# Every fourth weight half of the expert stages is split by GpSimd, with a counter of its own

## The reference

```python
def hier_moe(x, w_group, b_group, w_router, b_router, w_gate, w_up, w_down):
    """Two-level routing: top-1 expert group, then top-2 experts inside it; gate = p_group * p_expert."""
    ...
    h = jax.nn.silu(jnp.einsum('td,edf->tef', xf, w_gate)) * jnp.einsum('td,edf->tef', xf, w_up)
    y = jnp.einsum('tef,efd->td', h * gates[:, :, None].astype(h.dtype), w_down)
    return y.reshape(B, S, D)
```

## Time and profile before

| | us |
|---|---|
| median of three runs | 1051.6 (1048.8 to 1054.5) |
| the profiled execution, whole | 1050.4 |
| its span in the trace | 1048.7 |
| TensorE busy | 982.3 (94% of the span) |
| DVE busy | 717.4 (68%) |
| ACT busy | 546.4 (52%) |
| GpSimd busy | 28.3 (3%) |
| first expert stage, in the trace | about 200 to 357 |
| second expert stage | about 507 to 664 |

### The profile page before, as it was taken

How to read it: one execution, slowest core, us unless ns; L and a number is a source line. 1 busy time by engine, 2 the same in 40 slices (tenths; PEclk the granted TensorE clock), 3 DMA queues, 4 the chain that set the end, 5 groups by cost and what they waited for, 6 DMA issues and landing times.

```text
span 1048.7 us, 15179 instructions
## 1 busy us (share of the span) xinstructions
PE 982.3 (94%) x5898; PEld 851.5 (81%) x5898; DVE 717.4 (68%) x865; ACT 546.4 (52%) x603; POOL 28.3 (3%) x65
## 2 busy tenths in 40 slices
PE   8999999999999999997899999997897899999987
PEld 8978988787787798876787787787785899998876
DVE  4788787788689765527888788744554765666575
ACT  4655653467667535551676676433453544444431
POOL 5000010000000000000000000000000000000000
PEclk9999999899999999998999999998999899999999
DMA  9543327299699854412499699554305665555611
GB/s 313 195 162 121 122 93 229 79 324 351 218 364 345 285 195 160 128 42 80 161 326 361 219 345 376 197 166 139 115 7 176 217 199 182 179 173 189 230 51 41
DMA packets 151700, 205.86 MB, mean 196 GB/s; under 512 B 6736, under 2 KB 122960, under 8 KB 151632
## 3 DMA queue, kind: packets, MB, share of 16 engines
q1 hardware_dynamic: 150768, 204.24, 58.2%
q10 hardware_dynamic: 864, 0.70, 0.2%
HBM read 203.86 MB, written 1.05 MB: 195 GB/s over the span
## 4 chain that ended last, share of the span: by engine, by line
PE 77%; DVE 11%; ACT 5%; issue 4%; DMA 2%; POOL 0%; SPq 0%; DVEq 0%; ACTq 0%
PE psum L599 75%; DVE w_lo L1820 5%; ACT w_hi L1387 3%; ACT arena L1387 1%; DVE xt_lo L1837 1%; DMA x_res<-in_x 1%; DMA raw<-in_ffn_w_up 1%; PE psum L704 1%; ACT xt_hi L1387 1%; DVE x_res L2063 1%; PE psum L1036 1%; DVE stats L2068 1%; POOL rstd L462 0%; ACT mt_hi L1387 0%; DVE x_res L2086 0%
## 5 line engine op out<-in xcount | busy, mean ns | idle before, releaser
L1820 DVE TENSOR_TENSOR w_lo<-raw,w_hi 128x2048 fp32r<-128x2048 f32 x184 | 418.2, 2289 | 106.2 <-ACT w_hi L1387 104.2
L1387 ACT ACTIVATE w_hi<-raw 128x2048 fp32r<-128x2048 f32 (+1 forms) x186 | 353.1, 1905 | 116.6 <-PE psum L599 69.8
L599 PE MATMUL psum<-xt_hi,w_hi 128*128 128x256 f32 x704 | 201.7, 287 | 1.8 <-DVEq L2465 1.4
L599 PE MATMUL psum<-xt_hi,w_lo 128*128 128x256 f32 x704 | 199.9, 284 | 0.0
L599 PE MATMUL psum<-xt_lo,w_hi 128*128 128x256 f32 x704 | 199.8, 284 | 0.0
L599 PE MATMUL psum<-w_hi,xt_hi 128*128 128x512 f32 (+1 forms) x432 | 172.2, 399 | 10.3 <-issue 5.7
L599 PE MATMUL psum<-w_hi,xt_lo 128*128 128x512 f32 (+1 forms) x432 | 168.1, 389 | 0.0
L599 PE MATMUL psum<-w_lo,xt_hi 128*128 128x512 f32 (+1 forms) x432 | 167.7, 388 | 0.0
L599 PEld LDWEIGHTS psum<-xt_hi,w_hi 128*128 128x128 f32 x704 | 136.0, 193 | 3.0 <-issue 3.0
L599 PEld LDWEIGHTS psum<-xt_hi,w_lo 128*128 128x128 f32 x704 | 136.0, 193 | 0.0
L599 PEld LDWEIGHTS psum<-xt_lo,w_hi 128*128 128x128 f32 x704 | 135.8, 193 | 0.0
(11 more groups left out here) (246 smaller groups left out, 1220.0 us busy)
## 6 DMA issues: line engine op xcount, KB each, us to landing
raw<-in_w_gate SPq DMA_DIRECT2D x64, 512.0 KB, 4.9
raw<-in_w_up SPq DMA_DIRECT2D x64, 512.0 KB, 6.1
raw<-in_w_down SPq DMA_DIRECT2D x64, 512.0 KB, 5.7
raw<-in_ffn_w_up SPq DMA_DIRECT2D x44, 512.0 KB, 4.6
raw<-in_a_w_in SPq DMA_DIRECT2D x26, 512.0 KB, 6.5
raw<-in_attn_w_in SPq DMA_DIRECT2D x24, 512.0 KB, 5.6
raw<-in_ffn_w_down SPq DMA_DIRECT2D x22, 512.0 KB, 4.3
raw<-in_w_o SPq DMA_DIRECT2D x16, 512.0 KB, 4.6
```

What stands on the lines that cost most here:

```text
L599: return pe.matmul(o, l, r, start=start, stop=stop, skip_group_check=skip)
L1387: return act.activation(o, i, f, **kw)
L1820: return dve.tensor_tensor(w_half(h, w_lo), w_half(h, raw), w_half(h, w_hi).bitcast(F32), ALU.subtract).then_inc(lo_split, 1)
```

## The change

In each expert stage the halves n3, n7 and n11 of every group (`(h - AT[e]) % 4 == 3`) are split by GpSimd, by the same subtraction, and DVE leaves them out. That is 12 halves a layer, 24 in all, of the 96 of the two stages. GpSimd raises `pool_split`; `lo_split` now counts only DVE's halves, and every wait of TensorE and SP is on one or the other counter with a number worked out by `pool_at` and `lo_at`. All of the 24 lie in slot 0 or slot 2 of the ring, one slot per layer. SP's loop over the groups of a layer is written out.

```diff
+def by_pool(h):
+    return any(0 <= h - AT[e] < GROUPS * PER_G and (h - AT[e]) % 4 == 3 for e in ("E0", "E1"))
...
+            def raw_free(m):
+                if by_pool(m):
+                    sp.wait_ge(pool_split, pool_at(m))
+                else:
+                    sp.wait_ge(lo_split, lo_at(m))
...
-                with sp.Fori(0, GROUPS) as g:
+                for g in range(GROUPS):
...
-                        sp.wait_ge(lo_split, g * PER_G + (h + n - RING + 1))
+                        raw_free(h + g * PER_G + n - RING)
...
+            def expert_halves(layer):
+                for h in range(AT[f"E{layer}"], AT[f"E{layer}"] + GROUPS * PER_G):
+                    if by_pool(h):
+                        pool.wait_ge(hi_split, h + 1)
+                        pool.wait_ge(half_used, h - RING + 1)
+                        pool.tensor_tensor(w_half(h, w_lo), w_half(h, raw), w_half(h, w_hi).bitcast(F32),
+                                           ALU.subtract).then_inc(pool_split, 1)
...
+                if m in (0, 2):
+                    expert_halves(m // 2)
...
+                    def group_half(h):
+                        if by_pool(h):
+                            pe.wait_ge(pool_split, of_group(i, q, pool_at(h), PER_G_POOL))
+                        else:
+                            pe.wait_ge(lo_split, of_group(i, q, lo_at(h), PER_G_LO))
...
-                            dve.wait_ge(half_used, of_group(i, q, h - RING + 1, PER_G))
-                            split_half(h, of_group(i, q, h + 1, PER_G))
+                            if mark[0] >= PER_G or not by_pool(h):
+                                dve.wait_ge(half_used, of_group(i, q, h - RING + 1, PER_G))
+                                split_half(h, of_group(i, q, h + 1, PER_G))
```

More of the change, by code:

```diff
@@ L114, with pool_at, lo_at @@
 _unit("O21", AT["O2"], 4, [2, 3], "v")
+def by_pool(h):
+    return any(0 <= h - AT[e] < GROUPS * PER_G and (h - AT[e]) % 4 == 3 for e in ("E0", "E1"))
+def pool_at(h):
+    return sum(by_pool(m) for m in range(h + 1))
+def lo_at(h):
+    return h + 1 - pool_at(h)
+PER_G_POOL = PER_G // 4
+PER_G_LO = PER_G - PER_G_POOL
 def drained_by(name, who):
@@ L251, in build @@
         lo_split = sem("lo_split")
+        pool_split = sem("pool_split")
         half_used = sem("half_used")
@@ L295, in put @@
                 if h >= RING:
-                    sp.wait_ge(lo_split, h - RING + 1)
+                    raw_free(h - RING)
                 send(h % RING, make(raw[:, h % RING, :]))
@@ L468, in _ @@
                 power(n, slice(4 * b, 4 * b + 4))
-            for _ in range(6):
+            for m in range(6):
                 for b in range(TB):
@@ L619, in fm_half @@
                 if h:
-                    pe.wait_ge(lo_split, h + 1)
+                    pe.wait_ge(lo_split, lo_at(h))
                 fm_products(h, banks[0], xh, xl, s, after)
@@ L1018, in gate_up @@
                             h = base + G_AT[j] + half
-                            pe.wait_ge(lo_split, of_group(i, q, h + 1, PER_G))
+                            group_half(h)
                             wh, wl = (w_half(h, w).rearrange("p (k n) -> p k n", k=4) for w in (w_hi, w_lo))
@@ L1346, in up_pair @@
                 for q in range(2):
-                    pe.wait_ge(lo_split, h + q + 1 if i is None else i * 4 + (h + q + 1))
+                    pe.wait_ge(lo_split, lo_at(h + q) if i is None else i * 4 + lo_at(h + q))
                     fm_products(h + q, 2 * (j % 2) + q, xt_hi, xt_lo)
```

## The result

The changed kernel takes **1082.4 us** (median, 1080.0 to 1083.8) against 1050.3 for the kernel before (1048.8 to 1054.5) in runs beside each other. The ratio is 1.0297, with a 95% interval of 1.0259 to 1.0335: 3% slower, some 32 us. The sign was forecast, the time was not: 1064.6 had been predicted, with a range up to 1078.

A forecast was written before the change was run, and what follows sets the result against it. TensorE, busy 94%, was taken as the bound, with DVE's n8 split as every group's hinge. Delays of n8 summed to 6.5 us a layer, 13.0 in all, on the median 1051.6: 1064.6 us, range 1050.5 to 1078.

The forecast's parts named there:

- The hinge: In every group, the end of DVE's n8 split sets TensorE's start of gate_up(3), 0.83 us later; delay passes one for one.
- The exclusion holds the other way too: A GpSimd split reading SBUF also blocks DVE's next split, for up to 4.3 us; the trace showed only GpSimd waiting.
- t = 4.3 us: Assumed time of one split on GpSimd, against DVE's 2.29 us; range 3.4 to 5.1.
- Raw slots, "I count 0": GpSimd returns raw slots about 2 us or more later, but the transfer queue stays fed; counted as 0.
- The late issue still finds a half in flight: When SP issues a transfer late, the half ahead is still being transferred, so the queue stays fed; argued against transfer delay.
- Why n3 and n11 cost nothing more: n3's delay is covered by 0.7 us before TensorE asks; n11, last in a group, has more time than n7.
- `hidden` and `h_rest` aren't touched: These DVE instructions read psum, so GpSimd's SBUF reads do not exclude them.
- Rival C: Late raw slots run the transfer queue dry, up to 2.0 us for each of 24 halves; 1077 to 1090; 14%.
- B: GpSimd does not block DVE when it came first, so n8 keeps its place; 1051 to 1053; 18%.
- D: GpSimd does not block DVE, and DVE's freed time reaches a wait of TensorE; 6 us faster, 1045; 4%.

The follow-up runs named there:

- write-only kernel: Against the changed kernel, GpSimd's split replaced by three memsets of the same slot that read nothing from SBUF, lo parts zero; 1059.0 us, ratio 1.0069 against the kernel before.

## Why the prediction was wrong, point by point

- **The hinge** (gate_up(3) starts 0.83 after n8 ends, n8's delay goes through one for one): right. In the changed kernel n8 ends at 262.79 and TensorE starts at 263.62, 0.83 later, and n8 moved behind gave 16 us back.
- **The exclusion holds the other way too**: right, and was the one assumption without a row. It is shown by the 4.60 and 2.93 us splits that end 2.1 us after GpSimd, and by 2.29 us beside memsets. The Trainium skill (SBUF — State Buffer, Who interferes with whom) had it in both halves: reads against reads, no conflict for a DVE split beside a GpSimd that only writes. The traces agree on both. The same section of the Trainium skill says of DVE's two-port modes, not of this kind of split, that whichever engine issues first holds the ports for the whole instruction; that it is so for the split too is shown here by the ends 2.1 us after GpSimd's.
- **t = 4.3 us**: undersized. A split that doesn't have to wait takes 4.6 us (4.60 and 4.61 in the rows above). With 4.62 the working gives 1.8, 1.7, 2.8 and 1.75 us for the four groups, 8.1 a layer and 16.2 in all, where 18.0 was measured before gate_up(3). As a formula the step stands; by its own inputs it was 3.2 us short.
- **Raw slots, "I count 0"**: wrong. In the sum before gate_up(3) it shows once: the fourth group of the second layer lost 3.8 us instead of 1.75, as its transfers came late. "The late issue still finds a half in flight" was false there and in the kernel with n3 and n11. The write-only kernel, in which DVE's splits aren't held up, puts all that hangs on GpSimd's length, `place` included, at 7 us.
- **"Why n3 and n11 cost nothing more"**: right for n11 (1053.1 us, ratio 1.0013), wrong for n3. The two without n7 cost 14 us, by late transfers, by `place` and by the clock behind the gaps.
- **The step that failed is a term that the sum put at nothing**: it took a matmul's duration for fixed. Every term was idle time, "one for one", and none asked what the longer idle stretch does to the matmuls behind it. It cost 9.5 us behind gate_up(3), and 8 us came back by filling the stretch. The rest of the miss is in the points above and below: 5 us before gate_up(3) (18.0 instead of 13.0) and 3.1 behind it. The clock stood at 0.99 and 1.00 in the stages, but the trace of before did show what can follow a gap, at the very end of the first stage, where the scatter of the fourth group waits for `xt_lo`:

```profile
356.83 0.47 PE L599 MATMUL psum<-xt_hi,perm_t 128*128 128x512 f32 x1 [2.10 <-DVE xt_lo L1837]
...
357.43:360.13 2.70, 2.70 (x8) 2.12 (x8) 1.44 (x3) 1.04 (x1) 0.00 (x0) 0.50 1.10 347
```

  Behind 2.10 us of idle time the matmuls stand 0.43 us apart at a granted clock of 0.50, where they stand 0.23 apart otherwise. The forecast made gaps of some 3 us out of 1.5 and could have read the price here.
- **"`hidden` and `h_rest` aren't touched"** was right, and the list was incomplete: `place` is a DVE instruction in the same queue, reads and writes SBUF, and stands beside n11. It cost 3.4 us before down(2) in the two layers, about 3 with the slow down(2) behind it and what a later wait gave back.
- **Rival C** (transfers) gave 1077 to 1090 and so the right number, by luck for the most part. Its reason, late transfers at every turn, shows in one of the eight groups before gate_up(3), with 2 us; the other seven follow from t. B (n8 in time beside a running n7) and D (faster) are out.

## What to carry to other kernels

Before a piece of work goes from DVE to an idle GpSimd, write down what DVE has queued beside it: in these traces only instructions that read psum and at most one SBUF tensor went on unhindered; two-input SBUF instructions stopped for as long as GpSimd read, and `place`'s kind (SBUF to SBUF, one input) stopped beside its writes as well. If a saturated TensorE waits behind one of them, price the gap as idle time, and look in the traces for whether matmuls behind such a gap are slow, which is a second price. And look which half of a pattern is moved, not how many: n11 cost nothing, n7 some 2 us each.

## What the runs showed of the hardware

- A GpSimd subtraction of two 128x2048 fp32 tensors takes 4.6 us where it doesn't wait, against 2.29 on DVE; a memset of that size 1.81. The Trainium skill's 4497 ns (GPSIMD Engine Reference, Elementwise — side-by-side cycle accounting) is within 3% of it.
- A DVE instruction that is held up counts as busy. Here a mean that rose from 2289 to 2441 ns was contention, not work: beside GpSimd's memsets it was 2289 again.
- `place`'s instructions (one SBUF input, SBUF output, fp32) were held up by GpSimd's reads and by its pure writes, 3.88 and 2.96 us for four instead of 1.10.
- The granted clock fell to the 1.2 GHz level behind idle stretches of TensorE of 3.0 to 5.0 us in the changed kernel, but also behind 2.03 there (down(2), second group of the first layer), behind 2.1 in the kernel before, and behind 1.9 and 2.2 in the kernel with n3 and n11. It didn't fall behind 2.8 us in one group of the changed kernel (second layer, third group), nor behind the 2.98 of the last row shown among the experiments. Where it fell, gate_up(3) took 6.9 to 8.5 us instead of 5.5. The length of the gap alone doesn't decide, and what does was not found out.
